# VectorE's startup order, the place of two mail groups, and two moves around the decode keys, in a single-core decoder layer

## The reference, cut to what matters

```
u = rms_norm(h, g_pre)
A | B | C = u @ w_in        # one combined projection, 24 tiles of 128 columns here, plus the branch gates
A: native sparse attention, 8 heads in 2 groups. Three branches over the same queries:
   compressed: every 32 keys (values) summed with weights w_cmp_k (w_cmp_v); softmax with a T5 bias
   selected:   the 16 best blocks of 64 by the compressed probabilities (forced: first and last two)
   window:     the last 512 keys
   o = sum over branches of sigmoid(gate) * o_branch;  a = o * silu(z_a)
B: u = val * sigmoid(gate); c = causal depthwise convolution of width 31;
   cn = (c - mean) * rsqrt(var + eps) over each group of 64 channels, gain and bias; b = (silu(cn) @ w_pw) * silu(z_b)
C: causal convolution of width 4, two gates, h_t = a_t h_(t-1) + sqrt(1 - a_t^2) i_t x_t;  c = h * silu(z_c)
h = h + rms_norm(concat(a, b, c) @ w_out, g_post)
```

## Time and profile before

| | us |
|---|---|
| median of 3 runs | 998.63 |
| their range | 995.54 to 999.33 |
| the profiled execution | 993.99 |
| its span | 992.2 |

### The profile page before, as it was taken

The page is one execution under the profiler, slowest core; times in us unless marked ns, Lnnn a source line. Parts: engine busy times, 40 slices in busy tenths (PEclk is TensorE's granted clock), DMA queues, the critical chain, the costliest instruction groups (busy, mean ns, idle before and its releaser), DMA issues.

```text
span 992.2 us, 16009 instructions
## 1 busy us (share of the span) xinstructions
PE 903.3 (91%) x6261; PEld 574.2 (58%) x6261; DVE 598.4 (60%) x1136; ACT 372.1 (37%) x846; POOL 106.7 (11%) x104
## 2 busy tenths in 40 slices
PE   3999999999699999997999999987778999699997
PEld 2565665666356666666667776765645666444443
DVE  4378788999978896965465566556633444312222
ACT  4210235210012201135877777756535655311010
POOL 1011210000010110100102112130241231000000
PEclk9999999999899999999999999999899999999999
DMA  8333552422043355452700000000046984912111
GB/s 302 141 127 106 191 188 75 60 60 65 25 160 125 127 190 181 155 233 69 250 1 2 2 2 2 2 2 2 1 152 265 366 311 163 352 64 83 66 54 53
DMA packets 31678, 118.34 MB, mean 119 GB/s; under 512 B 3385, under 2 KB 11723, under 8 KB 22923
## 3 DMA queue, kind: packets, MB, share of 16 engines
q0 software_dynamic: 9360, 68.16, 18.8%
q1 hardware_dynamic: 18621, 43.39, 12.4%
q10 hardware_dynamic: 3623, 5.76, 2.8%
HBM read 108.33 MB, written 13.29 MB: 123 GB/s over the span
## 4 chain that ended last, share of the span: by engine, by line
PE 51%; DVE 24%; DVEq 7%; DMA 6%; issue 4%; ACT 4%; SPq 2%; ACTq 0%; PEldq 0%; PEld 0%; POOL 0%
PE PS L1992 11%; DVE main L649 8%; PE PS L838 6%; PE PS L1551 5%; PE PS L1541 5%; PE PS L1569 4%; DVE main L611 4%; PE PS L811 3%; DMA main<-in_cmp_k_dram,row 3%; PE PS L1839 3%; PE PS L1588 3%; PE PS L1856 3%; DVE main L608 2%; PE PS L1867 2%; ACT main L1381 2%
## 5 line engine op out<-in xcount | busy, mean ns | idle before, releaser
L838 PE MATMUL PS<-main 128*128 128x352 f32 (+1 forms) x1056 | 328.7, 470 | 0.0
L838 PEld LDWEIGHTS PS<-main 128*128 128x128 f32 x1056 | 200.8, 191 | 119.9 <-issue 2.5
L1381 ACT ACTIVATE main<-PS,main 128x512 f32<-128x512 f32 (+3 forms) x192 | 103.9, 562 | 44.7 <-DVE main L1410 20.7
L1992 PE MATMUL PS<-main 128*128 128x512 f32 x256 | 112.2, 600 | 0.0
L434 ACT ACTIVATE main<-PS 128x384 f32<-128x384 f32 x24 | 11.7, 489 | 214.1 <-PE PS L838 205.6
L649 DVE SCALAR_TENSOR_TENSOR main<-main,par 128x1022 f32<-128x1022 f32 (+16 forms) x66 | 83.8, 1270 | 5.3 <-issue 0.4
L1992 PEld LDWEIGHTS PS<-main 128*128 128x128 f32 x256 | 49.1, 193 | 61.6 <-issue 61.6
L608 DVE TENSOR_TENSOR main<-main 128x1024 f32<-128x1024 f32 x64 | 75.4, 1219 | 14.2 <-DMA main<-in_cmp_k_dram,row 9.8
L1373 ACT ACTIVATE main<-PS 128x512 f32<-128x512 f32 (+1 forms) x138 | 69.1, 598 | 29.5 <-PE PS L1551 29.5
L1551 PE MATMUL PS<-cst,main 128*128 128x128 f32 x528 | 71.5, 280 | 9.1 <-ACT main L1381 9.0
L611 DVE TENSOR_TENSOR main<-main 128x1024 f32<-128x1024 f32 (+2 forms) x96 | 75.0, 781 | 7.2
(11 more groups left out here) (316 smaller groups left out, 1050.9 us busy)
## 6 DMA issues: line engine op xcount, KB each, us to landing
main<-in_w_tiles_dram SPq DMA_DIRECT2D x24, 512.0 KB, 3.6
out_dram<-main SPq DMA_DIRECT2D x18, 256.0 KB, 2.0
main<-in_x_prompt_dram SPq DMA_DIRECT2D x8, 512.0 KB, 10.0
main<-in_w_out_dram SPq DMA_DIRECT2D x1, 4096.0 KB, 18.0
main<-in_x_prompt_dram SPq DMA_DIRECT2D x16, 256.0 KB, 3.1
out_dram<-main SPq DMA_DIRECT2D x4, 512.0 KB
diag<-in_win_k_dram SPq DMA_DIRECT2D x8, 256.0 KB
diag<-in_win_v_dram SPq DMA_DIRECT2D x8, 256.0 KB
```

The costliest lines, as they stand in the source:

```text
L838: last = pe.matmul(bank(3 * s + j)[:, 0:w], ring[:, s, k * P:(k + 1) * P], xT[:, k, t0:t0 + w], start=(k == 0), stop=(k == KD - 1))
L1381: last = act.activation(prob[:, k % 2, g, h * nk_ * P:(h + 1) * nk_ * P], score_set(k, g)[:, h * nk_ * P:(h + 1) * nk_ * P], ACT.Exp, scal ...
L1992: last = pe.matmul(bank(2 * (m % 2) + h), proj[:, MIX[k], n * P:(n + 1) * P], wo[:, k, h * 512:(h + 1) * 512], start=(k == 0), stop=(k == ...
```

## The change

Five edits, all in order only; no instruction is added or removed.

- Startup: the parameters are ACT's first DMA; `dve_startup` comes first on VectorE, with its wait for the parameters ahead of n == 2; the rows are worked out after evac(2) and the tables after evac(4).
- The mean mails go from the last pieces of project 6 to after pieces 0, 1 and 2 of project 7 (the eighth pair), and the variance mails from there to after its pieces 3, 4 and 5. ACT's list follows.
- The first piece of project 10 goes ahead of the turned keys.
- VectorE's compress pieces 25 to 30 each go one place forward, so that piece 25 stands ahead of the first prompt scores and only piece 31 is left ahead of the pairs.
- ACT's masks go ahead of the second half of the silu of z_a.

```diff
@@ act_startup
+            act.dma_start(par[:, :], dram["parameters"]).then_inc(ld_par, 16)
             for u in range(4):
                 act.dma_start(rel[...], dram["rel_bias"]).then_inc(ld_rel, 16)
...
-            act.dma_start(par[:, :], dram["parameters"]).then_inc(ld_par, 16)
@@ dve_startup
-            dve.wait_ge(ld_par, 16)
...
             for n in range(11):
+                if n == 2:
+                    dve.wait_ge(ld_par, 16)
                 if n < 9:
                     square(n)
                 if 1 <= n < 10:
                     scale(n - 1)
                 if n >= 2:
                     evac(n - 2)
+                if n == 4:
+                    dve_rows(dve)
+                if n == 6:
+                    dve_tables(dve)
@@ scalar
-            act_project(act, 6, 0, 1)
+            act_project(act, 6)
             act_squares(act, 0, 4)
-            act_project(act, 6, 1, 2)
+            act_project(act, 7, 0, 1)
             act_squares(act, 4, 6)
-            act_project(act, 7, 0, 1)
+            act_project(act, 7, 1, 2)
             act_var(act)
-            act_project(act, 7, 1, 2)
...
             act_project(act, 11, 1, 2)
+            act_masks(act)
             act_branch_a_gates(act, 2, 4)
-            act_masks(act)
@@ vector
-            dve_tables(dve)
-            dve_rows(dve)
             dve_startup(dve)
...
             dve.drain().then_inc(SEM["bc_done"], 1)
+            dve_compress(dve, 25, 26)
             dve_prompt_scores(dve, M_PC)
-            dve_compress(dve, 25, 26)
+            dve_compress(dve, 26, 27)
             dve_prompt_scores(dve, M_PC + 1)
...
-            dve_compress(dve, 30, 32)
+            dve_compress(dve, 31, 32)
@@ tensor
-            pe_project(pe, 6, 0, 4)
-            pe_mean(pe, 0, 2)
-            pe_project(pe, 6, 4, 5)
-            pe_mean(pe, 2, 4)
-            pe_project(pe, 6, 5, 6)
-            pe_mean(pe, 4, 6)
+            pe_project(pe, 6)
             for q in range(3):
                 pe_project(pe, 7, q, q + 1)
+                pe_mean(pe, 2 * q, 2 * q + 2)
+            for q in range(3):
+                pe_project(pe, 7, q + 3, q + 4)
                 pe_var(pe, 2 * q, 2 * q + 2)
-            pe_project(pe, 7, 3, 6)
...
+            pe_project(pe, 10, 0, 1)
             pe_decode_keys(pe)
-            pe_project(pe, 10, 0, 1)
             pe_prompt_blocks(pe)
```

More of the change, by code:

```diff
@@ L2172, in _ @@
             dve.drain().then_inc(SEM["bc_done"], 1)
+            dve_compress(dve, 25, 26)
             dve_prompt_scores(dve, M_PC)
-            dve_compress(dve, 25, 26)
+            dve_compress(dve, 26, 27)
             dve_prompt_scores(dve, M_PC + 1)
             dve_decode_queries(dve)
-            dve_compress(dve, 26, 27)
+            dve_compress(dve, 27, 28)
             dve_prompt_scores(dve, M_PC + 2)
-            dve_compress(dve, 27, 28)
+            dve_compress(dve, 28, 29)
             dve_prompt_scores(dve, M_PC + 3)
             dve_prompt_cmp(dve)
-            dve_compress(dve, 28, 29)
+            dve_compress(dve, 29, 30)
             dve_decode_scores(dve)
@@ L2185, in _ @@
             dve_decode_norm(dve)
-            dve_compress(dve, 29, 30)
+            dve_compress(dve, 30, 31)
             dve_select(dve)
             dve_new_values(dve)
-            dve_compress(dve, 30, 32)
+            dve_compress(dve, 31, 32)
             dve_pairs_prepare(dve)
```

## The result

| | before | after |
|---|---|---|
| median of 20 runs | 996.18 us (981.20 to 1000.85) | 996.25 us (992.74 to 1001.51) |
| span of the profiled execution | 992.2 us | 995.0 us |

The ratio of after to before is 1.006, 95% interval 1.0033 to 1.0087: some 6 us slower by it, while the two medians are equal. The ratio leaves out runs more than 1.5% above a kernel's fastest, and because before has one run at 981.20 this drops ten of its twenty runs and none of after's. Over all runs the means are 994.8 and 996.7, a ratio of 1.002, so how much slower the changed kernel is, if at all, is not settled by its time. I had said 999.0 as a median, 993 to 1004 as a range, and no change by 0.5% as likeliest.

The account below looks back on a forecast made before the run. PE, busy 903.3 of 992.2 us, has idle time to draw on, but VectorE's chain paces the middle. 0.45 + 1.8 - 2.4 + 1.8 - 1.3 = +0.35 us: 994.3 profiled, 999.0 as median (4.6 added), range 993 to 1004.

Parts of the forecast that it names:

- Startup: First chunks: 2.4 us won, 2.84 us of tables not hidden, so chunk(0,1) +0.45 us, plus 1.8 for the clock: +2.25.
- The wait that takes the place of the one removed: Middle: PE, 12 us ahead, stands still some 7 us at the third pointwise mail, until VectorE frees its bank.
- The last variance mail: Middle: the last variance pair comes behind six pieces of project 7 instead of three, 2 us later (1.8 to 2.7).
- In between nothing waits: VectorE takes the means as early as today: Mean and variance mails: VectorE takes means after its compress pieces and frees the variances' banks before PE comes; no wait.
- Turned keys: Project 10's first piece fills PE's wait; its second starts 2.4 us earlier (-1.2 to -4.4), less 1.8 for the clock.
- Masks: ACT's masks ahead of the silu: the 2.70 us before line 1261 shrink to 0.5, gaining 1.3 us (0.4 to 2.2).
- Compress pieces: VectorE's pieces moved forward fill its 7 us wait for the first prompt scores; cost nothing, one piece less ahead of attention.
- 12 to 13 us: PE time gained by the start of project 8: waits of 7.67 and 1.5 us and 1.8 us of half clock removed.
- rival 4: Startup: PE stays at half clock through chunk(0,1), turn 6 and chunk(1,1); +8.9 us, median 1007.5; chance 0.11.
- rival 3: Middle: PE, not VectorE, paces, so the 12 us or so stay; -11.5 us, median 987; chance 0.08.
- rival 1: The clock stays up at both pauses, startup and turned keys; -3.25 us, median 995.4; chance 0.21.
- rival 2: Startup: the tables hide, and the clock there stays up too; -4.3 us, median 994.3; chance 0.08.

Follow-up runs that it names:

- g0: The kernel before, unchanged, traced a second time; waits 2.5 us at the convolutions, last variance 230.6 us behind line 769.
- e4: The kernel before with only ACT's masks moved ahead of the second half of the silu; ratio 1.0005 (0.9964 to 1.0046).
- f2: The changed kernel with 34 extra identity transposes filling PE's pause ahead of chunk(0,1); ratio against before 1.0046 (1.0013 to 1.0079).
- e1: The kernel before with the startup edits alone; ratio 1.0027 (0.9992 to 1.0061).
- e2: The kernel before with only the mean and variance mails moved as in the change; ratio 1.0105 (1.0049 to 1.0161), medians 1003.17 and 993.85 us.
- g2: f4 with the mean and variance mails moved by two pieces instead of three; median 977.61 us, ratio against before 0.9875.
- f3: The changed kernel with pointwise mails 3 to 6 one piece further back and project 10's first two pieces ahead of the keys; ratio against before 1.0037.
- f4: The changed kernel with tables after evac(5), f3's order and three of four silu tiles early; median 986.22 us, ratio against before 0.9954.
- g3: g2 with the last two pairs of variance mails posted without a piece between them; median 976.96 us, ratio against before 0.9857.

## Why the prediction was right, and what was mis-sized

The forecast was no change beyond 0.5%, the gains given back by the tables, by VectorE's chain and by the clock. By the medians (996.18 and 996.25) it held; by the ratio of 1.006 it is missed by a tenth of a per cent, on the slower side. The mechanism held, but the closeness of the time, 2.8 us above the median measured, is in part luck. By the stretches up to the attention +3.24 us came out where I had summed +0.35, which is 2.9 too little; and the 4.6 us that I added for the median of three runs were 2.4 too much, since with twenty runs the median of before is 996.18 and not 998.63. The two errors go opposite ways.

- **Startup: right.** Said: chunk(0,0) at 19.7, chunk(0,1) at 40.5 after 4.3 us of idle time, 1.8 us for the clock. Seen: 19.88, 39.92, 4.41 and 1.9. In all +1.80 to line 769 (said 2.25).
- **The wait that takes the place of the one removed: right.** Said 7 us at the third group of line 892, seen 5.97; said that VectorE's chain is fixed, and it took 83.9 to 86.2 us from the last variance to the turned keys in the twelve traces in which PE waits there.
- **The last variance mail: mis-sized.** Said +2.0 (1.8 to 2.7), measured +2.9 against the first trace, of which 1.6 are a fall of the clock behind the small products after the startup (the window 67.50 of after at 0.62), which no bound of mine held, and 1.3 the step itself. But the first trace is not typical. Against the four other traces of the old place (230.5 on average) the six of the change's place (236.1) are 5.6 us later. The step that failed is "In between nothing waits: VectorE takes the means as early as today": in the changed kernel VectorE waited 4.80 us for the first mean. It took it 207.7 us behind line 769, against 206.5 in the first trace and 202.1 to 203.2 in the four others. In the first trace VectorE was through with the convolutions 4 us late, after 9.9 us of waits for gathers, and so a place three pieces later looked free.
- **Turned keys: the mechanism right, the clock mis-sized.** The edit was said to bring -4.4 before its clock price of 1.8; seen in all -1.1 against the first trace. The clock took 1.8 on the scores and 1.6 on the piece, 3.4 in place of 1.8. Against g0, where the clock falls at this place with the old order too, it is -2.8. One sign did not come: project 10's second piece was to start 2.4 us earlier less the startup's shift, and it started 2.0 us later (392.25 against 390.23), 0.2 beyond that shift.
- **Masks: mis-sized.** -1.3 said, -0.3 seen; PE at half clock paces the natural turns (e4 against f2).
- **Compress pieces: right** in that they cost nothing; VectorE's wait of 7.75 us for the first scores is gone; what they bring was not tried alone.

Two figures of the working do not follow from their own terms. PE's gain in the middle, "12 to 13 us", adds up to 11.0 from the three terms named. And the 1.5 us from which rival 4 is said to be slower than before has no base, as the sum stands at +0.35 without it.

Against a typical execution of before the terms are +2.0, +5.6, -2.8 and -0.3: +4.5 us, within the ratio's +3.3 to +8.7, though the equal medians show none of it. Nor do the parts add up at the end: the ratios of e1 to e4 multiply to 1.014, the whole has 1.006, and most of the excess is e2's, from six runs. The rivals: PE as the pacer (rival 3) is shown false by e2. The clock staying up (rival 1) and hidden tables (rival 2) by e1. Rival 4's half clock lasted 3.9 us (0.71 over 6.8) and not through chunk(1,1).

What stays open is why executions differ by 5 us in the waits for the cached gathers and by more than 10 us in the decode part; and why before has runs below 989 us which after lacks.

## What to carry to other kernels

When work is moved to fill a wait, ask whose chain the moved mail starts, and count it from that engine's side: taking away a wait of TensorE gained nothing here, a mail five microseconds late cost five. Take the length of a wait from more than one execution before placing something behind it by its length. Put small helper work behind the last item that a waiting engine needs, not ahead of it, and price a pause of TensorE with the half clock that may follow.

## What the runs showed of the hardware

The clock fell in places without a long pause. After 1.50 us of idle time chunk(0,1) took 5.00 us in one execution of before and 6.69 in another of the same code, and 6.70 and 6.69 in e4 and g2. Behind the small products of lines 769 to 781, without any pause over 0.3 us, the clock was at full speed in before and averaged 0.62 in after. The two places go together: in the six traces in which chunk(0,1) took 6.69 us or more (g0, e1, e4, after, f3, g2) the piece behind the small products took 6.47 to 6.88 us, and in the eight others, f2 with its filled pause among them, 5.33. So a fall at the startup's pause came with a second one 20 us later, worth 1.6 to 1.7 us; why is not shown. And after 4.45 us of waiting in f3 it stayed at 1.2 GHz (0.50) through 11.2 us of nearly unbroken work that began with 32 narrow score products (7.09 us; the same in f4, after 4.46). Narrow products alone do not do it: the same 32 took 3.79 us in g2, after 1.70 us of waiting, and in g3. Windows of a trace tell what it did once, not what it will do.

The Trainium skill, TensorE: Matmul & The Clock Gate, "Why this matters for your kernels", advises against idle gaps between bursts of matmuls. Where the gap was over 4 us (after, e1, f3) the traces agree each time; f2 shows it with the gap filled. Below 3 us the traces show both outcomes.
